# An encoder layer on one core: the paired down product in both feed-forward parts, and a weight rounding moved on ScalarE

## What is computed

```python
mod = silu(c) @ ada_w + ada_b                       # sh1, sc1, g1, sh2, ... g3
h = modulate(rmsnorm(x, ffn1_norm), sh1, sc1)
x = x + 0.5 * g1 * (silu(h @ wg1) * (h @ wu1)) @ wd1      # hidden width 2816
h = modulate(rmsnorm(x, mix_norm), sh2, sc2)
x = x + g2 * token_mixing(h)
h = modulate(rmsnorm(x, ffn2_norm), sh3, sc3)
x = x + 0.5 * g3 * (silu(h @ wg2) * (h @ wu2)) @ wd2
x = rmsnorm(x, final_norm)
```

## Time and profile before

| | us |
|---|---|
| three runs | 3032.97, 3033.53, 3038.99 |
| median | 3033.53 |
| the profiled execution, device time | 3033.41 |
| its span | 3031.6 |
| first part: rounds 0 and 1 of half 0 | 76.67 to 183.26 |
| its loops (rounds 2 to 9, and 13 to 20) | 183.26 to 552.11, 698.12 to 1066.97 |
| first part, rounds 11 and 12 (start of half 1) | 599.45 to 698.12 |
| attention | about 1120 to 2009 |
| second part, loops (pairs 1 to 4) | 2113.79 to 2465.30, 2612.79 to 2964.91 |

### The profile page before, as it was taken

The page is one execution under the profiler, slowest core; times in us unless marked ns, Lnnn a source line. Parts: engine busy times, 40 slices in busy tenths (PEclk is TensorE's granted clock), DMA queues, the critical chain, the costliest instruction groups (busy, mean ns, idle before and its releaser), DMA issues.

```text
span 3031.6 us, 49322 instructions
## 1 busy us (share of the span) xinstructions
PE 2915.9 (96%) x16297; PEld 2687.0 (89%) x16297; DVE 1684.7 (56%) x2862; ACT 1501.3 (50%) x2515; POOL 2065.9 (68%) x1046
## 2 busy tenths in 40 slices
PE   7899999999999999997989999999999998999998
PEld 3899999999999988885656667989999998999998
DVE  5766664676666656886543332275443466544545
ACT  7433333533333366766767775444444455444444
POOL 1766666776666663334547666678898887989894
PEclk9999999999999999998999999999999999999999
DMA  8233332133333234557313225441212242221224
GB/s 279 77 101 100 104 107 80 56 91 111 100 100 104 77 114 145 137 147 177 103 51 91 71 78 151 121 138 61 84 55 83 65 134 92 62 84 55 83 70 160
DMA packets 368360, 310.76 MB, mean 103 GB/s; under 512 B 22012, under 2 KB 324463, under 8 KB 368239
## 3 DMA queue, kind: packets, MB, share of 16 engines
q1 hardware_dynamic: 365102, 307.62, 33.8%
q10 hardware_dynamic: 3136, 1.57, 0.2%
HBM read 257.00 MB, written 52.13 MB: 102 GB/s over the span
## 4 chain that ended last, share of the span: by engine, by line
PE 63%; POOL 16%; issue 9%; DVE 4%; DMA 3%; ACT 3%; SPq 2%; ACTq 0%; POOLq 0%; DVEq 0%
PE PS L3135 9%; PE PS L3137 9%; PE PS L3136 9%; POOL W_lo L2520 8%; PE PS L444 7%; PE PS L445 7%; PE PS L446 7%; POOL quart L2533 4%; DMA quart<-in_ffn_wu 2%; PE PS L1533 1%; PE PS L1478 1%; PE PS L1535 1%; PE PS L1534 1%; POOL XT_r L1770 1%; PE PS L3189 1%
## 5 line engine op out<-in xcount | busy, mean ns | idle before, releaser
L3135 PE MATMUL PS<-SL,W_hi 128*128 128x384 f32 x2112 | 715.5, 339 | 34.0 <-POOL W_lo L2520 16.8
L3136 PE MATMUL PS<-SL,W_hi 128*128 128x384 f32 x2112 | 709.6, 336 | 0.0
L3137 PE MATMUL PS<-SL,W_lo 128*128 128x384 f32 x2112 | 709.4, 336 | 0.0
L1980 DVE SCALAR_TENSOR_TENSOR XT<-PS,mod,XT 128x384 f32<-128x384 f32 (+1 forms) x880 | 440.1, 530 | 278.9 <-PE PS L446 200.8
L2440 POOL TENSOR_TENSOR W_lo<-quart,W_hi 128x1024 fp32r<-128x1024 f32 x132 | 326.5, 2482 | 316.3 <-ACT W_hi L2434 316.3
L2520 POOL TENSOR_TENSOR W_lo<-quart,W_hi 128x1024 fp32r<-128x1024 f32 x192 | 469.7, 2467 | 55.2 <-ACT W_hi L2515 55.1
L3135 PEld LDWEIGHTS PS<-SL,W_hi 128*128 128x128 f32 x2112 | 399.3, 189 | 43.7 <-POOL W_lo L2520 20.5
L1770 POOL TENSOR_TENSOR XT_r<-XT,XT_r 128x512 fp32r<-128x512 f32 x224 | 286.8, 1286 | 178.6 <-ACT XT_r L1622 178.2
L3136 PEld LDWEIGHTS PS<-SL,W_hi 128*128 128x128 f32 x2112 | 399.3, 189 | 1.0 <-issue 1.0
L3137 PEld LDWEIGHTS PS<-SL,W_lo 128*128 128x128 f32 x2112 | 399.5, 189 | 0.0
L2515 ACT ACTIVATE W_hi<-quart 128x1024 fp32r<-128x1024 f32 x192 | 200.6, 1059 | 277.8 <-PE PS L3191 124.0
(11 more groups left out here) (337 smaller groups left out, 6860.1 us busy)
## 6 DMA issues: line engine op xcount, KB each, us to landing
quart<-in_ffn_wg SPq DMA_DIRECT2D x176, 256.0 KB, 3.1
quart<-in_ffn_wu SPq DMA_DIRECT2D x176, 256.0 KB, 3.5
down<-in_ffn_wd SPq DMA_DIRECT2D x48, 512.0 KB, 3.3
quart<-in_ffn_wd SPq DMA_DIRECT2D x80, 256.0 KB, 2.9
raw<-in_w_out SPq DMA_DIRECT2D x30, 512.0 KB, 4.3
ada_w_sb<-in_ada_w SPq DMA_DIRECT2D x6, 2048.0 KB, 17.8
SLf<-in_ada_w SPq DMA_DIRECT2D x64, 192.0 KB, 2.7
ada_r<-in_ada_w SPq DMA_DIRECT2D x64, 192.0 KB, 3.0
```

What stands on the lines that cost most here:

```text
L1980: mm = dve.scalar_tensor_tensor(out=xt, in0=PS[:, bank, a - c * NB:b - c * NB], scalar=hgate[:, g, m, s:s + 1], in1=xt, op0=ALU.mult, op1= ...
L3135: pe.matmul(out, w_hi, m_hi, start=j in PRODUCT_OPENS and kp == 0, stop=False, skip_group_check=True)
L3136: pe.matmul(out, w_hi, m_lo, start=False, stop=False, skip_group_check=True)
L3137: mm = pe.matmul(out, w_lo, m_hi, start=False, stop=kp == 3, skip_group_check=True)
```

## The change

1. The first feed-forward part takes the stages of the second: `spots` serves both, with halves h = 0 and 1 as well. The rounds, with their own functions, go. Pairs 1 to 4 remain a loop (on SP, pairs 1 to 3, and pair 4 is unrolled).
2. ACT's `spot_hi(act, N, 1)` at the end of GA and GB now stands behind the copies of T1, T3 and T2.
3. The gated tiles are kept otherwise: DVE does the second and the fourth product twice (`exact=True` writes the unrounded one to SBUF), ACT's raw copies of B22 and T2 go, T3 and T2 are made in other PSUM banks, and T4's rounded parts live in a parked row of x.
4. The 16 turns of the modulation stand in GA and GB of the pairs 1 to 4 of h = 0 and 1, with a ring of three slots (AR = 3). SP issues six of the loads ahead of the next stage's quarter A11 and two behind it. PE's small matmuls stand behind the product T3, in the middle of the stage.
5. Parking of x comes at the end of the first GA's loads (before: ahead of them), and x is fetched back in two steps, after the 16th and the 28th step of the last DN.

```diff
-AR = 4
+AR = 3
@@ ACT, gate_up
                 silu_act(act, S, 1)
                 spot_hi(act, N, 0)
                 made_hi_act(act, S, B11)
-                raw_act(act, S, B11)
+                raw_act(act, S)
                 silu_act(act, S, 2)
-                spot_hi(act, N, 1)
                 made_hi_act(act, S, T1)
                 made_hi_act(act, S, T3)
                 made_hi_act(act, S, T2)
-                raw_act(act, S, T2)
+                spot_hi(act, N, 1)
@@ made_hi_act
-                act.wait_ge(t_made, S.made(T_ORDER.index(j) + 1))
+                act.wait_ge(t_made, S.made({T1: 1, T3: 3, T2: 3, T4: 4}[j]))
@@ SP, spot
-                if S.first:
-                    park(S.h)
-                N = S.ahead()
+                N, last = S.ahead(), S.kind == DN and isinstance(S.p, int) and S.p == PAIRS - 1
+                for k in range(6) if S.ada() else ():
+                    ada_load(sp, S, k)
                 spot_load(sp, N, A11Q, sum_ready, S.sums(4))
+                for k in range(6, KD) if S.ada() else ():
+                    ada_load(sp, S, k)
                 spot_load(sp, N, A21Q, unit_ready, S.unit(5))
                 spot_load(sp, N, A22Q, unit_ready, S.unit(6))
+                if last:
+                    unpark(sp, S.h, 0)
                 spot_load(sp, N, A12Q, unit_ready, S.unit(7))
+                if S.first:
+                    park(sp, S.h)
@@ ada_load (its wait: sum k - AR of the same turn is done)
+            sp.wait_ge(ada_chain, S.ada_chain(max(k - AR + 1, 0)))
@@ ada_sum
+            if k == 0 and S.kind == GA:
+                dve.wait_ge(d_acc, S.behind().down(26))
+            if k == 0 and S.kind == GB:
+                dve.wait_ge(st_hid, S.behind().ready(PN))
@@ DVE, gate_up
+                turned, before = S.first and S.h % 2, 4 if S.kind == GA else 3
+                for k in range(before) if S.ada() else ():
+                    ada_sum(dve, S, k)
                 add_dve(dve, S, 0)
...
                     mult_dve(dve, S, 0)
                     made_lo_dve(dve, S, B22)
+                if S.ada():
+                    for k in range(before, KD):
+                        ada_sum(dve, S, k)
+                    ada_fold(dve, S)
+                    ada_mods(dve, S)
                 add_dve(dve, S, 1)
                 add_dve(dve, S, 2)
...
                 mult_dve(dve, S, 1)
                 made_lo_dve(dve, S, B11)
-                mult_dve(dve, S, 2)
+                mult_dve(dve, S, 2, True)
                 t_dve(dve, S, T1)
                 t_dve(dve, S, T3)
+                t_dve(dve, S, T2)
                 made_lo_dve(dve, S, T1)
                 made_lo_dve(dve, S, T3)
-                t_dve(dve, S, T2)
                 made_lo_dve(dve, S, T2)
@@ DVE, tail
+                mult_dve(dve, G, 3, True)
                 mult_dve(dve, G, 3)
@@ PE, gate_up
                 for j in range(PN):
                     spot_product(pe, S, j)
+                    if S.ada() and j == T3:
+                        ada_reduce(pe, S)
@@ the engines' lists (PE as an example)
-            st_pe(pe)
+            ffn_pe(pe, 0)
             mix_pe(pe)
             attention_pe(pe)
             wo_pe(pe)
-            ffn2_pe(pe)
+            ffn_pe(pe, 1)
```

More of the change, by code:

```diff
@@ L2282, in spots @@
                 dn(Spot(DN, h, 0))
-                with eng.Fori(1, PAIRS) as p:
+                with eng.Fori(1, looped) as p:
+                    g(Spot(GA, h, p))
+                    g(Spot(GB, h, p))
+                    dn(Spot(DN, h, p))
+                for p in range(looped, PAIRS):
                     g(Spot(GA, h, p))
@@ new lines, in wait_used, with spot_hi @@
+        def wait_used(eng, S, u):
+            if S.kind == DN:
+                eng.wait_ge(d_steps, S.down(4 * u + 4))
+            else:
+                eng.wait_ge(st_steps, S.step(2 * u + 2 if u < PN else SN))
+        def spot_hi(act, S, u):
+            if u >= PN:
+                act.wait_ge(down_landed[u - PN], S.down_row(16))
+            elif u in (0, 1, 5):
+                act.wait_ge(quart_landed[UNIT_FROM[u]], S.quart(32))
+            else:
+                act.wait_ge(sum_ready, S.sums({2: 1, 3: 3, 4: 2, 6: 4}[u]))
+            if u >= WS:
+                wait_used(act, S, u - WS)
+            elif S.first and S.h == 0:
@@ L2547, in spot @@
                     pool.wait_ge(unit_ready, S.unit(PN + 1))
-                if S.kind != SO or S.h == 2:
+                if S.ahead() is not None:
                     spot_sum(pool, S.ahead(), 0)
                     spot_lo(pool, S.ahead(), 0)
-            spot_lo(pool, Spot(GA, 2, 0), 0)
-            spots(pool, spot, spot, spot)
+            S0 = Spot(GA, 2 * f, 0)
+            spot_lo(pool, S0, 0)
+            if f == 0:
+                for no in range(3):
+                    spot_sum(pool, S0, no)
+                spot_lo(pool, S0, 1)
+            spots(pool, f, spot, spot, spot)
         BX, BY, BZ, BV = 0, 2, 4, 6
@@ L2606, in keep_act @@
             act.wait_ge(st_steps, S.step(product_step((B11, T2, T3)[which], role)))
-            if which == 0:
-                act.wait_ge(part_added, S.added(role - 3))
-            if which == 1:
-                act.wait_ge(part_added, S.added(role - 1))
+            if which < 2 and S.first and S.h > 0:
+                act.wait_ge(part_added, S.added(role + (-3, -1)[which]))
+            if which < 2 and not S.first:
+                act.wait_ge(t_made, S.made(-1 + which))
             if which == 2:
@@ L2661, in gate_up @@
             def gate_up(S):
-                N = S.ahead()
+                N, turned = S.ahead(), S.first and S.h % 2
                 if S.kind == GB:
                     tail(S)
-                elif S.first and S.h == 3:
+                elif turned:
                     spot_hi(act, S, 1)
@@ L2674, in gate_up @@
                 spot_hi(act, S, 3)
-                if S.first and S.h == 3:
-                    op_hi_act(act, 3, T3)
+                if S.first and S.h == 0:
+                    for j in (T4, B22):
+                        op_hi_act(act, 0, j)
+                if turned:
+                    op_hi_act(act, S.h, T3)
                 spot_hi(act, S, 4)
@@ L2684, in gate_up @@
                 keep_act(act, S, 3)
-                if S.first and S.h == 3:
+                if S.first and S.h != 2:
                     silu_act(act, S, 0)
@@ L2715, in single @@
             def single(S):
-                R, turns = S.round(), S.h == 2
+                turns, leaves, h = S.h % 2 == 0, S.h == 1, S.h + 1
+                if leaves:
+                    sums_act(act, 1, 0, (0, 2))
                 spot_hi(act, S, 2)
@@ L3110, in st_product @@
[L3110 to L3127 removed]
+            spots(dve, f, gate_up, down, single)
```

1017 lines of the change are left out of this document (362 added, 655 removed).

## The result

The changed kernel takes **3153.7 us** (median of four runs, 3146.3 to 3158.6) against 3035.1 for the kernel before in the same comparison: a ratio of 1.0387, with a 95% interval of 1.0366 to 1.0409. Slower, as forecast, but by 118.6 us and not by 75.6, and 28.7 above the end of the range. The profiled execution has a span of 3154.3 us, 122.7 more than before.

A forecast was written before the change was run, and what follows sets the result against it. TensorE was taken as the bound, with GpSimd its equal in the second part (slack 0.64 us). Terms 26.7 + 32.4 - 1.0 + 3.9 + 13.6 = +75.6 on 3033.4 gave 3109 us, range 3026 to 3125.

The forecast's parts named there:

- the fetch of x: End of a half: x, fetched in two 8.7 us pieces, the first ahead of a weight quarter; nothing to +4, taken as nothing.
- the late fold: First part's GA and GB: late modulation sums hold up T4, losing 2.85 us in GA and 4.45 in GB.
- Part 1, ScalarE's order: GA and GB: late rounding makes GpSimd's unit 1 2.15 late, TensorE waits; second-part pairs 90.6, +26.7 us there.
- Part 2, the paired product: First part: 24 matmuls less in each of 10 pairs, 4.16 us each; GpSimd's 33 instructions for 26 covered down to the slack.
- Part 3, the modulation: First part's loops: loads 6 and 7 land late, so TensorE waits for the fold before T4; pairs of 96.25, +32.4 us.
- Part 5, the clock: Matmuls behind the 16 new waits: half the waits followed by half-clock matmuls, 1.7 us each; +14, ends 0 and +27.
- Part 4, the edges: First pairs of halves 0 and 1: -1.0 and +3.9 us; the fetch of x taken as nothing.
- PE as the bound: Rival, both parts: GpSimd catches up and the fold is in time, so TensorE stays the bound; 2997 us, chance 0.17.
- Order alone: Rival: only ScalarE's order costs, as loads land early enough or VectorE's sums overlap; 3056 us, chance 0.20.
- Modulation alone: Rival: only the modulation costs, 2.25 us lost twice a first-part pair; 3028, or 3041 with half of the clock, chance 0.10.
- landing: Load 6 in the first part's turns: taken to land 3.2 us after issue, between 2.4 and 4.1; ends -13 and +14.

The follow-up runs named there:

- E1: The changed kernel with ScalarE rounding the next stage's unit 1 ahead of the copies of T1, T3 and T2 again: 3057.5 us.
- E4: The changed kernel with unit 1's rounding ahead of the copies, all eight modulation loads ahead of A11, and x's first piece fetched behind quarter A12: 2999.1 us.
- E10: The changed kernel with modulation loads 6 and 7 between the two DMAs of quarter A11 instead of behind both: 3131.9 us.
- E2: The changed kernel with all eight modulation loads of a turn issued ahead of the next stage's A11 quarter: 3082.8 us.
- E9: The changed kernel with 11 useless 128x128 matmuls in TensorE's wait for the fold, with start=False: 3130.8 us.
- E3: The changed kernel with x's first piece fetched behind quarter A12 of the single round, not ahead of it: 3143.2 us.
- E8: The changed kernel with 20 useless 128x128 matmuls in TensorE's wait for the fold, with start=True: 3153.6 us.

## Why the prediction was wrong in size

The direction and the mechanism were right, three terms of the sum were mis-sized. By the spans the change cost 122.7 for 75.6. Of the 47.1 between them, the fetch of x, put at nothing, is 13, the late fold 11, and the clock 9; the rest is smaller pieces.

**Part 1, ScalarE's order: right.** Unit 1 at +0.2 behind the border, gaps in front of T2 and T3 and pairs of 90.6 were forecast. Measured: +0.19, the same gaps, pairs of 90.9 and 91.2. The second part's loops cost 12.3 and 12.8 for 10.9 and 10.3, the first pairs 2.3 and 2.2 for 3.0 and 2.5. E1 undoes it and nothing else, and the second part falls back to 87.6 and 87.8.

**Part 2, the paired product: right.** GpSimd's seven more instructions a pair are covered once unit 1 is in time: E4's two first loops are within 1.4 and 2.4 us of TensorE's pace.

**Part 3, the modulation: the chain right, one term mis-sized.** "Here two are ahead, so I take 3.2" is the step that failed. Load 6 took 3.65 in the mean, 7.2 us more over 16 turns, and its issue came 1.3 and not 1.1 behind sum 3, 2.8 us more. T4 starts 24.7 into GA and 25.6 into GB for the forecast 23.65 and 25.25, which is 11 in eight pairs. The text had named this end of the range itself (+14) and had taken the middle between two rows, when the row with transfers ahead (4.1, behind four weight pieces) was the nearer one. E10 shows that load 6's landing follows what stands ahead, E2 that nearly all of the wait for the fold hangs on where the two loads are issued.

**Part 5, the clock: mis-sized.** "I take half of them" failed: 14 of 16 waits were followed by slow matmuls, 22.5 for 13.6 (1.6 each). The waits were 3.0 in the mean and not 2.4 to 2.7, but that their length made the slow stretches more frequent isn't shown: in E10 they were 1.1 shorter and 14 of 16 were still followed by one. E9 shows the price, 20.7; why a given wait is followed by a slow stretch stays open. Forecast for the first loops 46.0, measured 70.4; of the surplus of 24.4, 11 is T4's later start, 8.9 the clock, 1.3 in DN, and most of the rest the first matmul behind each wait, which is late by itself.

**Part 4, the edges: wrong.** "Nothing to +4, taken as nothing, as the first piece is issued 12 us before the pair ends" failed twice. It asked when the pair ends, and not what is queued behind the piece: quarter A12, issued 1.3 later, from which ScalarE rounds unit 1 some 4 us ahead of the border. (The piece was issued 9.3 before the pair ended in the row above, and not 12.) And it was counted once, at most 4, for what happens at the end of every half. E3 shows 10.5, its trace 13.0 in three places. Some 5 us more lie in the start and in the stretch from half 1's single round to the end of attention; their cause stays open.

**The rivals.** PE as the bound did not happen, but is near to E4, in which three causes of delay are undone: 2999 for the 2997 worked out. That the totals meet is in part luck: the first loops gained 29.5 and not 33, the first pair of half 0 gained 7.5, and the start and attention lost 5. Order alone (3056) is what E2 left, which took 3083: some 15 of the difference is the fetch of x, some 10 the loops of both parts, whose pairs took 0.6 more than was worked out. Modulation alone (3028 to 3041) is what E1 left, which took 3057.5: its pairs in the first part took 94.5 for 91.9, which is 21, and the fetch of x some 13.

**The range** ended at 3125, and the forecast's own bounds at 3137. The terms with a known far end (landing +14, clock +13) both came out in its direction (11 and 9), and the range had cut that off. Even the far bound, 3137, has nothing for the fetch of x in it.

## What to carry to other kernels

A load that a fold in mid-stage needs must not stand on its queue behind a load that waits for something else: moving two issues by one line was worth 71 us here, and one line for one transfer another 10. When the feeder's slack against the bound engine is as small as here (0.64 us in a stage of 29.12), look at the one instruction on a third engine between them, and cost its lateness once for the border and once more for each wait that hangs behind it. Where two uncertain terms hang on the same wait, as its length and the clock behind it do here (E2 removes both), let the range hold both far ends together.

## What the runs showed of the hardware

- The clock isn't decided by the length of the idle time alone. Idle times of 3.30 in E3 and 2.61 in E1 were followed by no slow matmul, by the distances of the starts (a clock of 1.00 in the window behind E3's), while one of 1.62 in E10 was, by some ten (a clock of 0.60):

```profile
868.88 0.25 PE L532 MATMUL PS<-ada_part,fold 128*32 128x6 f32 x8 [3.30 <-DVE ada_part L515]
869.05:873.50 4.45, 4.45 (x33) 4.43 (x26) 2.53 (x7) 2.58 (x5) 3.88 (x2) 1.00 0.45 142
...
540.08 0.25 PE L532 MATMUL PS<-ada_part,fold 128*32 128x6 f32 x8 [1.62 <-DVE ada_part L515]
540.29:544.60 4.31, 4.31 (x22) 4.31 (x17) 2.53 (x7) 2.58 (x5) 3.85 (x2) 0.60 0.26 95
```

  In E2, E4, E8 and E9 there is no slow stretch in the first part's loops. In the kernel before, an idle time of 2.04 was free of it and one of 2.10 not the earlier trace rows.
- An f32 matmul of 128x128 is two rows in the trace, 0.112 apart: 20 are x40.
- Free columns of a PSUM bank are not free for a new sum. E8 and E9 write the same columns beside an open sum and differ else only in how often; with `start=True` the open sum's result changed, with `start=False` it did not. By the Trainium skill (PSUM — Partial Sum Buffer, The four PSUM rules) a second opening in the same bank clears the first sum's state, and that sum's next matmul overwrites. These runs agree in that the open sum is lost; the overwriting itself no run shows.
